# The second FFN matrix in another order of its seven products, its weight sums on GpSimd, and a finer wait for the first merge gates

## The reference

```
y = (sig(gA)*A + sig(gB)*B + sig(gC)*C) @ w_out ;  x = x + gate1 * RMSNorm(y)
x = x + gate2 * RMSNorm(SwiGLU(RMSNorm(x) * (1 + scale2) + shift2))

a, b = jnp.split(h @ w_ffn_in_l, 2, axis=-1)
x = x + gate2 * rms_norm((jax.nn.silu(a) * b) @ w_ffn_out_l, norm_g_l[3])
```

## Time and profile before

| | |
|---|---|
| median of 3 runs (lowest, highest) | 1809.89 us (1808.49, 1811.78) |
| profiled execution | 1809.75 us, span 1807.9 us |
| TensorE matmul, weight load: busy share of the span | 96%, 89% |
| VectorE, ScalarE, GpSimd: busy share | 48%, 35%, 22% |
| mean granted TensorE clock | 0.985 |
| DMA | 304.06 MB, mean 168 GB/s |
| loads of a 256 KB block of f: median from issue to landing | 5.1 us |

### The profile page before, as it was taken

How to read it: one execution, slowest core, us unless ns; L and a number is a source line. 1 busy time by engine, 2 the same in 40 slices (tenths; PEclk the granted TensorE clock), 3 DMA queues, 4 the chain that set the end, 5 groups by cost and what they waited for, 6 DMA issues and landing times.

```text
span 1807.9 us, 24605 instructions
## 1 busy us (share of the span) xinstructions
PE 1732.9 (96%) x9622; PEld 1611.4 (89%) x9622; DVE 865.1 (48%) x1405; ACT 627.4 (35%) x1109; POOL 404.4 (22%) x476
## 2 busy tenths in 40 slices
PE   6999999999999999989989899999999999999996
PEld 3899998979999999987978799999999999887885
DVE  4400002333334444446867965444444443588885
ACT  6311113232222222223656483222222223454442
POOL 0400001322122232343415253222222220000000
PEclk9999999999999999989999999999999999999998
DMA  9544445654355556688758232222222225698683
GB/s 352 209 169 152 165 155 191 223 191 139 128 177 185 171 190 203 208 220 253 251 170 252 93 119 75 73 74 71 72 73 74 73 73 177 189 312 257 176 272 119
DMA packets 164266, 304.06 MB, mean 168 GB/s; under 512 B 13257, under 2 KB 98060, under 8 KB 164154
## 3 DMA queue, kind: packets, MB, share of 16 engines
q1 hardware_dynamic: 120288, 171.01, 29.5%
q0 software_dynamic: 27536, 91.31, 15.5%
q10 hardware_dynamic: 16336, 40.29, 6.7%
HBM read 234.79 MB, written 67.82 MB: 167 GB/s over the span
## 4 chain that ended last, share of the span: by engine, by line
PE 79%; DVE 6%; DMA 5%; ACT 3%; issue 3%; POOL 2%; SPq 2%; ACTq 0%; DVEq 0%; POOLq 0%
PE bank L658 24%; PE bank L659 24%; PE bank L660 24%; DMA raw<-in_w_stream 1%; DVE w_lo L1891 1%; PE bank L899 1%; DMA mg<-z_scratch 1%; PE bank L1144 1%; PE bank L1147 1%; PE bank L1154 1%; PE bank L1162 1%; DMA ada_raw<-in_w_ada 1%; SPq L753 1%; POOL ya L2705 1%; DMA z_scratch<-z_st 1%
## 5 line engine op out<-in xcount | busy, mean ns | idle before, releaser
L658 PE MATMUL bank<-h_hi,w_hi 128*128 128x384 f32 x1080 | 375.9, 348 | 7.8 <-DVE h_lo L2487 5.1
L659 PE MATMUL bank<-h_lo,w_hi 128*128 128x384 f32 x1080 | 365.8, 339 | 0.0
L660 PE MATMUL bank<-h_hi,w_lo 128*128 128x384 f32 x1080 | 365.5, 338 | 0.0
L1891 DVE TENSOR_TENSOR w_lo<-raw,w_hi 128x1024 fp32r<-128x1024 f32 x152 | 201.8, 1329 | 271.4 <-ACT w_hi L1414 270.9
L658 PEld LDWEIGHTS bank<-h_hi,w_hi 128*128 128x128 f32 x1080 | 204.1, 189 | 24.9 <-ACT z_st L1473 10.1
L1414 ACT CAST w_hi<-raw 128x1024 fp32r<-128x1024 f32 x152 | 157.4, 1050 | 169.4 <-DMA raw<-in_w_stream 107.4
L659 PEld LDWEIGHTS bank<-h_lo,w_hi 128*128 128x128 f32 x1080 | 204.4, 189 | 0.1
L660 PEld LDWEIGHTS bank<-h_hi,w_lo 128*128 128x128 f32 x1080 | 204.0, 189 | 0.0
L658 PE MATMUL bank<-w_hi,a_hi 128*128 128x512 f32 x352 | 139.6, 397 | 4.3 <-DVE w_lo L2382 4.3
L659 PE MATMUL bank<-w_lo,a_hi 128*128 128x512 f32 x352 | 140.6, 399 | 0.0
L660 PE MATMUL bank<-w_hi,a_lo 128*128 128x512 f32 x352 | 139.8, 397 | 0.0
(11 more groups left out here) (344 smaller groups left out, 3445.8 us busy)
## 6 DMA issues: line engine op xcount, KB each, us to landing
raw<-in_w_stream SPq DMA_DIRECT2D x142, 512.0 KB, 4.5
raw<-in_w_stream SPq DMA_DIRECT2D x101, 256.0 KB, 5.8
z_scratch<-z_st ACTq DMA_DIRECT2D x44, 576.0 KB, 3.1
raw<-in_w_ada SPq DMA_DIRECT2D x35, 512.0 KB, 5.7
a_raw<-f_scratch SPq DMA_DIRECT2D x44, 320.0 KB, 4.8
mg<-z_scratch ACTq DMA_DIRECT2D x24, 576.0 KB, 6.7
a_raw<-f_scratch SPq DMA_DIRECT2D x33, 256.0 KB, 5.1
zt<-z_scratch POOLq DMA_DIRECT2D x27, 256.0 KB, 3.6
```

The source lines that it names most:

```text
L658: pe.matmul(out, a_hi, b_hi, start=start, stop=False)
L659: pe.matmul(out, a_hi, b_lo, start=False, stop=False)
L660: return pe.matmul(out, a_lo, b_hi, start=False, stop=stop)
L1891: dve.tensor_tensor(w_lo[:, slot], raw[:, slot], w_hi[:, slot].bitcast(F32), ALU.subtract).then_inc(s_wlo, 1)
```

## The change

The products are taken in the order 1, 7, 6, 5, 4, 2, 3. Product 1 loads its block of f into `S_ch` and the following ones form their sums from there, so each step of every product loads one block of f (products 7 and 5 had two) and only product 7 two blocks of weights (products 7 and 5 had two); `a_aux` is gone. The sums of weights (`b_sum`) are done by GpSimd instead of VectorE. The evacuation is rewritten for the new order (`fo_u2`, `fo_u4`): ScalarE's for two products, VectorE's for the rest, with one addition less per tile. In the last product the lone tile comes last instead of first, and half of its square is done ahead (`first_half_alone`). `o_square` writes to `T_ch` instead of `ob`, so that the wait for a free slot of `ob` moves from ScalarE to VectorE. The next tile's `fo_c12` is put between `o_scale` and `o_add`. In `e1(0)` ScalarE's wait for all of z becomes a wait in each of six `mg_load`s for the z block that it reads; GpSimd's wait for all of z stays.

```diff
-FO_ORDER = (1, 7, 5, 6, 4, 2, 3)
+FO_ORDER = (1, 7, 6, 5, 4, 2, 3)
-FO_ASUM, FO_BSUM, FO_TWO = (7, 5, 6, 3), (7, 5, 6, 4), (7, 5)
+FO_ASUM, FO_BSUM, FO_TWO = (7, 6, 5, 3), (7, 6, 5, 4), (7,)
-FO_TILES = (5, 6, 7, 8, ALONE, 0, 1, 2, 3)
+FO_TILES = (5, 6, 7, 8, 0, 1, 2, 3, ALONE)
...
-            if p == len(FO_ORDER) - 1:
-                return (4, 0, 1, 2, 3)
             return (0, 1, 2, 3, 4) if FO_ORDER[p] in FO_ALONE else (0, 1, 2, 3)
...
-                c0 = 640 * cols
-                sp.dma_start(a_raw[:, s % AR, 0:a_width(s)], f_dram[KF * rows + k, :, c0:c0 + a_width(s)]).then_inc(s_al[s % AR], 16)
-                if i in FO_TWO:
...
-                    sp.dma_start(a_aux[:, x % AX_R], f_dram[KF * rows + k, :, 640 * cols:640 * cols + 512]).then_inc(s_axl[x % AX_R], 16)
+                w = 640 if i in (1, 2, 3) else 512
+                dst = S_ch[:, k] if i == 1 else a_raw[:, s % AR, 0:w]
+                sp.dma_start(dst, f_dram[KF * rows + k, :, 640 * cols:640 * cols + w]).then_inc(s_al[s % AR], 16)
...
             def mg_load(x):
...
+                if 2 <= x < KT:
+                    z = Z1_UNITS + Z2_UNITS - KT + c
+                    act.wait_ge(s_zst[z % 2], 16 * (z // 2 + 1))
                 r = residue(g) * GW
                 act.dma_start(mg[x % MG], merge[c, :, :, r:r + GW]).then_inc(s_mg[x % MG], 16)
...
                     if x == 0:
                         for u in range(2):
-                            act.wait_ge(s_zst[u], 8 * (Z_COUNT - 1))
                             act.wait_ge(s_host[u], 16 * (5 - u))
...
             def a_sum(s):
...
-                out, left, right, op = {7: (a, a, a_aux[:, x], ALU.subtract), 5: (ch, a, a_aux[:, x], ALU.add),
-                                        6: (ch, ch, a, ALU.subtract), 3: (a, a, ch, ALU.subtract)}[i]
+                out, left, right, op = {7: (ch, ch, a, ALU.subtract), 6: (ch, a, ch, ALU.subtract),
+                                        5: (a, ch, a, ALU.add), 3: (a, a, ch, ALU.subtract)}[i]
...
             def fo():
                 for s in range(FO_FIRST, FO_STEPS):
                     a_sum(s + 1)
-                    b_sum(s + 1)
                     fo_low(s)
                     p, k = divmod(s - FO_EVAC, KF)
-                    if k == KF - 1 and p >= 3:
+                    if k == KF - 1 and p >= 2:
                         for t in range(4):
-                            (fo_sum, fo_c21, fo_c11)[p - 3](t)
+                            (fo_u2, fo_u4, fo_c21, fo_c11)[p - 2](t)
...
-                o_out(len(OUT_AT))
+                fo_c12(0)
                 for t in range(4):
-                    fo_c12(t)
-                    o_out(len(OUT_AT) + 1 + t)
+                    o_scale(4 + t)
+                    if t < 3:
+                        fo_c12(t + 1)
+                    o_add(4 + t)
+                o_scale(NT - 1)
+                o_add(NT - 1)
...
+            def b_sum(s):
+                i, k = fo_product(s), s % KF
+                left, ch = fo_raw(fo_load(s, 0)), T_ch[:, k]
+                for x in range(len(FO_B[i])):
+                    fo_landed(pool, fo_load(s, x))
+                right = fo_raw(fo_load(s, 1)) if i in FO_TWO else left
+                if i != 7:
+                    b = fo_step_of({6: 7, 5: 6, 4: 6}[i], k)
+                    pool.wait_ge(s_wlo, split_index(U_FO) + fo_operand(b) + 1)
+                    b_sum_done(pool, b)
+                out, a, b, op = {7: (ch, left, right, ALU.subtract), 5: (left, left, ch, ALU.subtract),
+                                 6: (ch, ch, left, ALU.add), 4: (ch, ch, left, ALU.subtract)}[i]
+                pool.tensor_tensor(out, a, b, op).then_inc(s_S, 1)
             def fo():
+                for s in range(FO_STEPS):
+                    if fo_product(s) in FO_BSUM:
+                        b_sum(s)
                 for r in range(NT - 1):
                     out_store(r)
```

More of the change, by code:

```diff
@@ L471, in build @@
         s_mxh, s_mxl = sem("mx_high"), sem("mx_low")
-        s_mg = [sem(f"merge_or_second_f_landed{i}") for i in range(MG)]
-        s_axl = s_mg
+        s_mg = [sem(f"merge_landed{i}") for i in range(MG)]
         s_ym, s_ya, s_yh, s_yl = (sem(n) for n in ("branches_gated", "y_summed", "y_high", "y_low"))
@@ L817, in b_load @@
                     second = e - 2 * RAW - fo_load(b, 0)
-                    if fo_product(b) not in (6, 4) and (fo_product(b), second) not in ((7, 0), (5, 1)):
+                    if fo_product(b) not in (6, 4) and (fo_product(b), second) != (7, 0):
                         sp.wait_ge(s_whi, split_index(U_FO) + fo_operand(b) + second + 1)
@@ L830, in a_load @@
                 i, k = fo_product(s), s % KF
-                rows, cols = FO_A[i][0]
+                rows, cols = FO_A[i]
                 if s == 0:
@@ L835, in a_load @@
                         sp.wait_ge(s_fs[g], 16 * PAIRS)
-                elif s >= AR:
+                elif s == KF:
+                    sp.wait_ge(s_fs[2], 16 * PAIRS)
+                if s >= AR:
                     step_done(sp, s - AR)
-                c0 = 640 * cols
-                sp.dma_start(a_raw[:, s % AR, 0:a_width(s)], f_dram[KF * rows + k, :, c0:c0 + a_width(s)]).then_inc(s_al[s % AR], 16)
-                if i in FO_TWO:
[L841 to L846, removed]
-                    sp.dma_start(a_aux[:, x % AX_R], f_dram[KF * rows + k, :, 640 * cols:640 * cols + 512]).then_inc(s_axl[x % AX_R], 16)
+                w = 640 if i in (1, 2, 3) else 512
+                dst = S_ch[:, k] if i == 1 else a_raw[:, s % AR, 0:w]
+                sp.dma_start(dst, f_dram[KF * rows + k, :, 640 * cols:640 * cols + w]).then_inc(s_al[s % AR], 16)
             def x1_load(r):
@@ L867, in _ @@
                 r = slice(512 * half, 512 * half + 512)
-                sp.wait_ge(s_oout, 3 * (NT - 1) + 3 + half)
+                sp.wait_ge(s_oout, 3 * (NT - 1) + 3 + 2 * half)
                 sp.dma_start(y_sample[0, tok:tok + P, r], ob[:, (NT - 1) % 2, r]).then_inc(s_last, 16)
@@ L1825, in fo_high @@
                 w = a_width(s)
-                act.copy(a_hi[:, a, 0:w], S_ch[:, s % KF] if i in (5, 6) else a_raw[:, a, 0:w]).then_inc(s_fh, 1)
+                act.copy(a_hi[:, a, 0:w], a_source(s, w)).then_inc(s_fh, 1)
                 if i in FO_BSUM:
@@ L1831, in fo_high @@
                 operand_free(act, o)
-                act.copy(fo_weights(o)[0], T_ch[:, s % KF] if i in (7, 6, 4) else fo_raw(fo_load(s, 0))).then_inc(s_whi, 1)
+                act.copy(fo_weights(o)[0], b_source(s)).then_inc(s_whi, 1)
                 if i == 7:
@@ L1862, in fo @@
                     p, k = divmod(s - FO_EVAC, KF)
-                    if k == KF - 1 and p < 3:
+                    if k == KF - 1 and p < 2:
                         for t in range(4):
@@ L2381, in fo_low @@
                 hi, lo = fo_weights(o)
-                dve.tensor_tensor(lo, T_ch[:, s % KF] if i in (7, 6, 4) else fo_raw(fo_load(s, 0)), hi.bitcast(F32),
+                dve.tensor_tensor(lo, b_source(s), hi.bitcast(F32),
                                   ALU.subtract).then_inc(s_wlo, 1)
```

125 lines of the change are left out of this document (66 added, 59 removed).

## The result

The changed kernel takes 1819.57 us (median of 8 runs, 1812.36 to 1822.53) against 1810.46 us for the kernel before (8 runs, 1807.19 to 1811.91). The ratio is 1.0047, 95% interval 1.0031 to 1.0062: **slower by some 8.5 us**, where the prediction had 1797.3 us. The profiled execution has a span of 1816.7 us against 1807.9.

What follows compares the result with a forecast made beforehand. TensorE, busy 96% of the span, was taken as the bound, so only its idle or low-clock time could pay. Second matrix 6.4, tail 3.1 and merge gates 3.0 made 12.5 us off 1809.75: 1797.3 us, range 1794.3 to 1804.5.

Steps and rivals of the forecast that it cites:

- Second matrix: Second FFN matrix: lighter loads end the 6.9 us lost to late `w_lo`, less 0.5 us idle: 6.4 us gained.
- The price of a GpSimd sum: Second FFN matrix: each sum of weights on GpSimd takes 1.07 us from VectorE, bounds 0 and 1.28.
- Products 6 and 5: three operations and a sum: Second FFN matrix: VectorE needs 2.87 us per step of these products against TensorE's 2.8.
- `w_lo` released late with GpSimd in front of it: Second FFN matrix: a trace sign that would show the forecast wrong; no size given.
- The slower case: Second FFN matrix: at 2 us a sum TensorE runs at VectorE's pace, about 1812 us in all; chance 0.07.
- Tail: After TensorE's last matmul: lone tile last, half its square done ahead; 3.1 us gained, bounds 2 and 3.2.
- G + 7.1: Tail: VectorE's chain ends 7.1 us after G, TensorE's end, before the change; forecast G + 4.0.
- Merge gates: First merge's gate loads: finer ScalarE wait brings 3.0 us, bounds -0.4 and 4.4.
- the stall moves one unit on: Branch products before the first merge: TensorE's wait moves from unit 3 to unit 4, which ends 0.4 us later.
- can only come from behind: First merge: DMA work moved earlier brings the fourth gates' `mg` forward 1.9 us, half of 3.8; 3.0 us gain counted.
- the fourth gates landing at 815 as now: First merge: a trace sign that would show the forecast wrong, the fourth gates coming no earlier than before.
- This rival: First merge: the stall only moves, since GpSimd's wait is untouched; 9.1 us gained in all, 1800.7 us; chance 0.22.

Runs made afterwards that it cites:

- run 1: Changed kernel with the sums of weights back on VectorE, all else as changed: 1802.85 us, ratio 0.9966 to the kernel before.
- Run 3: Changed kernel with GpSimd's sums of weights held back so that one falls on each VectorE step: 1805.58 us, ratio 0.9978 to the kernel before.
- Runs 4 and 5: Two of GpSimd's output stores issued by SyncE, in the changed kernel (1810.73 us, ratio 1.0005) and in the kernel before (1805.14 us, ratio 0.9977).
- run 6: Kernel before with only ScalarE's finer wait for the merge gates: 1811.56 us, ratio 1.0004.

## Why the prediction was wrong

*Second matrix: forecast 6.4 us off, measured 8.4 on.* Half of it held. The single loads remove the wait that they were meant to remove, and are worth 6.0 to 7.0 us with nothing in their way (run 1; counted with 6.9). The price of a GpSimd sum was right too: 1.07 counted, 1.10 measured. By the Trainium skill's rule ("SBUF — State Buffer", Who interferes with whom), whichever of the two engines comes second waits for the other's whole instruction. By it a sum, which takes 1.28 us alone, would cost up to that; the trace agrees that they take turns, at 1.10. **The step that failed is the count:** "Products 6 and 5: three operations and a sum", and for product 7 "then 3.30 - 0.60 + 1.07 = 3.77", are one sum on every step. The text says itself that GpSimd's sums run ahead, "since GpSimd needs only the landed load", and took it for a relief of product 4. Running ahead takes sums out of a later product and puts them on the steps of the product before, where VectorE has least in hand. And the limits were worked out for steps 28, 32, 35, 39 and 43 alone, with E as "the end of product 7 (step 21)", as if product 7 ended in time. By the prediction's own 3.77 us it did so with nothing to spare: eight steps from 1579.85 end at 1610.0, and TensorE stands from 1610.1. Eleven sums on seven steps made 3.7 us of it, products 6 and 5 went the same way. Run 3 shows what the bunching costs: with one sum per step the stage takes 248.9 us, so that 13.1 of the 15.4 us are the bunching and 2.3 the price of the sums, where the prediction counted 0.5. That is a gain of 4.7 us against the kernel before, inside the bounds of 1.5 and 6.9 that the prediction set. Its own sign of being wrong, "`w_lo` released late with GpSimd in front of it", is what the trace has.

*The slower case* (chance 0.07) had the right mechanism, VectorE's pace, with the wrong deciding point. "It decides from about 1.9 us a sum" is worked out for one sum per step; with eleven on seven the matrix was slower already at 1.1. No run varied the price.

*Tail: forecast 3.1 us off, measured 0.7.* VectorE's chain was well sized: its end came from G + 7.1 to G + 4.6 (forecast G + 4.0). The lone tile's reciprocal starts at 1804.72, G + 1.4 as forecast, in spite of two waits for stores of `ob` before it, 0.80 and 0.49 us; what was counted too short are the two halves behind it, 3.1 us instead of 2.6. (The terms for tile 3 add up to G + 0.7, not G + 0.85, which nothing else rests on.) **The step that failed** is the silent one from VectorE's last instruction to the end of the span, 7.0 us in the earlier trace rows against the span, taken as fixed. It is GpSimd's last store and its closing drain. The change brings GpSimd's last store only 0.6 us closer to TensorE's end (landed 5.4 us behind it before, 4.8 after). Runs 4 and 5 show both: moving two stores off GpSimd brings the span's end 6.1 and 4.3 us closer to TensorE's, and then the new tail is worth 2.5 us or a little more.

*Merge gates: forecast 3.0 us off, measured 0.3 on.* The prediction saw that "the stall moves one unit on" and put the loss at 0.4 us: so it came. **The term that failed** is the gain that "can only come from behind": 3.8 us of DMA time ahead of the fourth gates, "of which I count half". They were asked for some 0.7 us earlier, counted from the first branch product, and used 0.3 us later. Between the asking and the use the DMA engines are full in both kernels (share 1.04 and 1.05) and move 3.38 and 3.60 MB, of which 2.04 and 1.87 MB are of GpSimd's queue, whose loads stand behind its own wait. From the first branch product to the asking half a megabyte more of weights had been moved (0.52 MB of SP's loads before, 1.03 after), but 0.2 MB more of SP's loads came behind, and the engines stayed full. Where only the gate wait is changed (run 6) the fourth `mg` starts at 815.88: "the fourth gates landing at 815 as now" was the prediction's sign of being wrong. This rival had a chance of 0.22; the run without the rest (run 6) bears it out at 1.0004.

*Sum.* Counted by the profile: 1.1 (ahead of the second matrix, the gates' 0.3 in it) + 8.4 - 0.7 = 8.8 us slower; forecast 12.5 faster. The second matrix makes 14.8 of the difference, tail and gates 5.7, the stretch ahead of the second matrix without the gates the rest, 0.8.

## What to carry to other kernels

An operation that is moved to another engine can cost the engine that it left, when both work from SBUF: count how many of the moved operations fall on each step of the slower engine, not how many there are per step, since an engine that waits only for its loads runs ahead and bunches them on the product before. Check the lead at the end of every product with that count, the first one too. At the end of a program look at which engine closes last: here an output store issued by GpSimd put that engine's drain of 8.2 us behind its landing.

## What the hardware showed that was not expected

GpSimd's closing drain takes 8.23 us in the seven profiles in which it issues eight output stores and 8.07 us in the three in which SyncE issues two of the eight; in all ten it starts only once that engine has nothing left to wait for. What fills it no run shows. The drains of the other engines take 0.01 to 4.4 us. So in both kernels the span ended 8.7 us behind GpSimd's last landing.

A wait of TensorE costs more than the wait itself. From the matmul at 1608.25 to the one at 1620.03 the changed kernel loses 7.3 us against full rate (0.233 us a matmul), of which 4.3 are the two waits; most of the other 3.0 is the clock, at which thirteen matmuls start some 0.43 us apart behind the wait of 3.75 us (eleven in the earlier trace rows, counted there with 2.2 us). Behind the wait of 1.37 us at 1688.24 the granted clock stayed at 1.00 (1688 to 1692 us).
